# Seven block products instead of eight in a convolutional feed-forward down-projection, on one core

## The reference, cut to what matters

```
def conv_ffn(xn, buf, w_up, conv_w, conv_b, w_down):
    gu = xn @ w_up                       # (576, 1024) @ (1024, 6144)
    g, u = gu[..., :D_FF], gu[..., D_FF:]
    gc, new_buf = causal_dwconv(g, buf, conv_w, conv_b)   # width 3
    return (jax.nn.silu(gc) * u) @ w_down, new_buf        # (576, 3072) @ (3072, 1024)
x = x + conv_ffn(rmsnorm(x), ...)
```

## Time and profile before

| | |
|---|---|
| median of 3 runs | 1947.13 us (1945.86 to 1948.13) |
| the profiled execution | 1946.94 us, its span 1945.1 us |
| busy, PE / DVE / ACT / POOL | 98% / 55% / 39% / 36% |
| mean granted TensorE clock | 0.997 of full |
| loads and stores | 131.47 MB, mean 68 GB/s |

### The profile page before, as it was taken

How to read it: one execution, slowest core, us unless ns; L and a number is a source line. 1 busy time by engine, 2 the same in 40 slices (tenths; PEclk the granted TensorE clock), 3 DMA queues, 4 the chain that set the end, 5 groups by cost and what they waited for, 6 DMA issues and landing times.

```text
span 1945.1 us, 36321 instructions
## 1 busy us (share of the span) xinstructions
PE 1910.0 (98%) x13285; PEld 1840.1 (95%) x13285; DVE 1071.3 (55%) x1846; ACT 757.0 (39%) x1508; POOL 701.3 (36%) x688
## 2 busy tenths in 40 slices
PE   7999999999999999999999999999989999999998
PEld 7886679999999999999999999999989999999998
DVE  3677755556555655478435325439855852542541
ACT  4555655555455554331112111247653211121121
POOL 3340013433222233443333333366544343333331
PEclk9999999999999999999999999999999999999999
DMA  5320001311111110223322223232222322322222
GB/s 149 66 56 3 25 23 44 81 35 38 44 38 37 32 46 26 71 77 86 85 78 86 82 81 86 81 104 77 66 73 77 87 80 83 86 78 84 86 76 91
DMA packets 253078, 131.47 MB, mean 68 GB/s; under 512 B 43073, under 2 KB 250754, under 8 KB 252882
## 3 DMA queue, kind: packets, MB, share of 16 engines
q1 hardware_dynamic: 252514, 128.56, 23.8%
q10 hardware_dynamic: 444, 1.29, 0.2%
HBM read 126.21 MB, written 3.61 MB: 67 GB/s over the span
## 4 chain that ended last, share of the span: by engine, by line
PE 86%; DVE 9%; ACT 2%; issue 2%; DMA 1%; DVEq 0%; POOL 0%; SPq 0%; ACTq 0%; POOLq 0%
PE ps L200 18%; PE ps L203 18%; PE ps L201 17%; PE ps L1225 7%; PE ps L1223 7%; PE ps L1224 7%; PE ps L1253 3%; PE ps L999 2%; PE ps L1190 2%; DVE arena L1867 1%; PE ps L232 1%; PE ps L1026 1%; PE ps L1015 1%; DVE arena L2123 1%; DVE split L1870 1%
## 5 line engine op out<-in xcount | busy, mean ns | idle before, releaser
L200 PE MATMUL ps<-split,whi 128*128 128x288 f32 x3024 | 889.4, 296 | 11.1 <-DVE split L273 4.3
L201 PE MATMUL ps<-split,whi 128*128 128x288 f32 x3024 | 885.6, 295 | 0.0
L203 PE MATMUL ps<-split,wlo 128*128 128x288 f32 x3024 | 856.2, 295 | 0.0
L194 POOL TENSOR_TENSOR wlo<-raw,whi 128x1024 fp32r<-128x1024 f32 x187 | 457.3, 2447 | 615.1 <-ACT whi L171 604.5
L200 PEld LDWEIGHTS ps<-split,whi 128*128 128x128 f32 x3024 | 568.8, 188 | 15.2 <-issue 11.9
L201 PEld LDWEIGHTS ps<-split,whi 128*128 128x128 f32 x3024 | 569.0, 188 | 0.4
L203 PEld LDWEIGHTS ps<-split,wlo 128*128 128x128 f32 x3024 | 556.2, 188 | 0.0
L171 ACT CAST whi<-raw 128x1024 fp32r<-128x1024 f32 x187 | 194.8, 1043 | 378.3 <-DMA raw<-in_ffn_w_up 225.9
L1223 PE MATMUL ps<-split,split 128*128 128x384 f32 x768 | 268.3, 349 | 0.0
L1473 DVE TENSOR_REDUCE ssq<-arena 128x16 f32<-128x1024 f32 x128 | 156.2, 1220 | 186.7 <-ACT arena L1335 186.7
L1225 PE MATMUL ps<-split,split 128*128 128x384 f32 x768 | 258.0, 336 | 0.0
(11 more groups left out here) (285 smaller groups left out, 2107.7 us busy)
## 6 DMA issues: line engine op xcount, KB each, us to landing
raw<-in_ffn_w_up SPq DMA_DIRECT2D x96, 512.0 KB, 3.7
raw<-in_ffn_w_down SPq DMA_DIRECT2D x48, 512.0 KB, 3.9
arena<-in_cache_ckv SPq DMA_DIRECT2D x128, 128.0 KB, 2.0
raw<-in_rec_w_in SPq DMA_DIRECT2D x16, 512.0 KB, 3.8
raw<-in_attn_w_o SPq DMA_DIRECT2D x8, 512.0 KB, 4.9
raw<-in_rec_w_out SPq DMA_DIRECT2D x8, 512.0 KB, 4.0
raw<-in_attn_w_down SPq DMA_DIRECT2D x7, 512.0 KB, 7.6
raw<-in_attn_w_uq SPq DMA_DIRECT2D x48, 64.0 KB, 2.1
```

Of the source, the lines that this page charges most:

```text
L194: pool.tensor_tensor(wlo[:, t % RING, :], raw[:, t % RING, :], f32(whi[:, t % RING, :]), ALU.subtract).then_inc(w_lo, 1)
L200: pe.matmul(o, wh, a, start=first, stop=False)
L201: pe.matmul(o, wh, b, start=False, stop=False)
L203: mm = pe.matmul(o, wl, a, start=False, stop=last)
```

## The change

The down stage takes its 8 tiles in 4 pairs. A pair is a product of 2 x 2 blocks: two output chunks by two halves of the eight inner chunks (`HK` = 4 each) against those halves by two token halves. Instead of eight block products of 12 matmuls it makes seven (Strassen's scheme in Winograd's form), out of sums of weight blocks and sums of `h` blocks:

- DVE makes four sums of weight blocks per pair (`pair_sums`), ACT their high parts (`pair_high`), DVE the low parts of three of them (`sums_low`), and POOL the low parts of the four half tiles that are used as they are or in place (`pair_low`).
- DVE makes four differences and sums of `h` per round (`first_operands`, `second_operands`), ACT the high parts of all seven, DVE the low parts. Before, DVE made both parts itself.
- PE runs the seven products in three banks (`pair_pe`); DVE adds a bank to `xT` while PE goes on, in 288-column adds, seven per pair (`pair_add`). The products of pair 0 that need the last round's `h` are put last.
- The order of the inner chunks in the up stage changes (a round makes chunk r and chunk r + 4), the sums of pair 0 stand in the last round of the up stage, and the loops over rounds on ACT and DVE are written out.
- Outside the block: the gate weights of the recurrent layer are loaded two tiles later and split behind that layer's first norm; `frow` moves; three semaphores are shared with others.

The diff, cut to its core (lines that are only "..." stand for what is left out):

```
+        def pair_of(l, t0, s, p):
+            return t0 + 16 + 2 * (p % 2), s * 6 + p // 2, l * PAIRS + s * 4 + p
...
+        def pair_sums(dve, l, t0, s, p):
+            t, it, n = pair_of(l, t0, s, p)
+            b = p % 2
+            dve.wait_ge(w_loaded[t % RING], loaded(t) + 16 * it)
+            dve.wait_ge(w_loaded[(t + 1) % RING], loaded(t + 1) + 16 * it)
+            a11, a12 = first_half(raw, t), second_half(raw, t)
+            a21, a22 = first_half(raw, t + 1), second_half(raw, t + 1)
+            dve.tensor_tensor(s_raw[b][:, 0, :], a21, a22, ALU.add).then_inc(f_sum, 1)
+            dve.tensor_tensor(a21, a11, a21, ALU.subtract).then_inc(f_sum, 1)
+            dve.wait_ge(f_sum, SUM0 + 4 * n + 1)
+            dve.tensor_tensor(s_raw[b][:, 1, :], s_raw[b][:, 0, :], a11, ALU.subtract).then_inc(f_sum, 1)
+            dve.wait_ge(f_sum, SUM0 + 4 * n + 3)
+            dve.tensor_tensor(s_raw[b][:, 2, :], a12, s_raw[b][:, 1, :], ALU.subtract).then_inc(f_sum, 1)
+        def pair_high(act, l, t0, s, p):
+            t, it, n = pair_of(l, t0, s, p)
+            b = p % 2
+            split_hi(act, t, it)
+            act.wait_ge(f_sum, SUM0 + 4 * n + 3)
+            if b == 0:
+                act.copy(s_hi0[:, 0:2, :], s_raw[b][:, 0:2, :]).then_inc(f_hi, 1)
+            else:
+                act.copy(s_hi1, s_raw[b][:, 0:2, :]).then_inc(f_hi, 1)
+            act.wait_ge(f_sum, SUM0 + 4 * n + 4)
+            act.copy(s_hi(b, 2), s_raw[b][:, 2, :]).then_inc(f_hi, 1)
+            split_hi(act, t + 1, it)
+        def pair_low(pool, l, t0, s, p):
+            t, it, n = pair_of(l, t0, s, p)
+            def half_low(half, u, s_):
+                pool.tensor_tensor(half(wlo, u), half(raw, u), f32(half(whi, u)), ALU.subtract).then_inc(s_, 1)
+            pool.wait_ge(f_sum, SUM0 + 4 * n + 4)
+            pool.wait_ge(w_hi, t + 1 + 4 * it)
+            half_low(first_half, t, f_lo)
+            pool.wait_ge(w_hi, t + 2 + 4 * it)
+            half_low(first_half, t + 1, f_lo)
+            half_low(second_half, t, w_lo)
+            half_low(second_half, t + 1, w_lo)
+        def sums_low(dve, l, t0, s, p):
+            t, it, n = pair_of(l, t0, s, p)
+            b = p % 2
+            for i in range(3):
+                dve.wait_ge(f_hi, HI0 + 2 * n + (1 if i < 2 else 2))
+                dve.tensor_tensor(s_lo_op[b][:, i, :], s_raw[b][:, i, :], f32(s_hi(b, i)), ALU.subtract).then_inc(f_slo, 1)
+        def pair_product(pe, bank, wh, wl, op, ks, first, last, resumed=True):
+            wh, wl = wh.rearrange("p (k n) -> p k n", n=P), wl.rearrange("p (k n) -> p k n", n=P)
+            for k in ks:
+                mm = product(pe, [ps[:, bank, 0:HT]], wh[:, k, :], wl[:, k, :], [t_hi_op[:, k, op, :]],
+                             [t_lo_op[k][:, op, :]], first and k == 0, last and k == HK - 1, resumed)
+            return mm
+        def pair_pe(pe, l, t0, s, p, between=None):
+            t, it, n = pair_of(l, t0, s, p)
+            b = p % 2
+            x, y, z = X_BANK[b], Y_BANK, Z_BANK
+            h0 = l * FC + s * TF
+            every = range(HK)
+            a11, a12 = [first_half(v, t) for v in (whi, wlo)], [second_half(v, t) for v in (whi, wlo)]
+            s3, a22 = [first_half(v, t + 1) for v in (whi, wlo)], [second_half(v, t + 1) for v in (whi, wlo)]
+            s1, s2, s4 = [(s_hi(b, i), s_lo_op[b][:, i, :]) for i in range(3)]
+            def up_done(k, second):
+                if p == 0:
+                    pe.wait_ge(S["h"], h0 + 2 * k + 1 + second)
+            up_done(HK - 1, False)
+            pe.wait_ge(f_lo, LO0 + 2 * n + 1)
+            pe.wait_ge(acc_free[1], (t + AOFF) // 2 + 2 * it) if b == 0 else \
+                pe.wait_ge(acc_free[0], (t + 1 + AOFF) // 2 + 2 * it)
+            pair_product(pe, x, *a11, B11, every, True, True, False).then_inc(f_ps, 1)
+            pe.wait_ge(f_slo, SLO0 + 3 * n + 1)
+            if b:
+                pe.wait_ge(f_ev, EV0 + 5 * n - 1)
+            pair_product(pe, z, *s1, T1, every, True, True, False).then_inc(f_ps, 1)
+            early = range(HK - 1) if p == 0 else every
+            up_done(HK - 2, True)
+            pe.wait_ge(f_slo, SLO0 + 3 * n + 2)
+            pe.wait_ge(f_ev, EV0 + 5 * n + 1)
+            mm = pair_product(pe, x, *s2, T2, early, False, True)
+            if p == 0:
+                pe.wait_ge(w_lo, t + 1 + 4 * it)
+                pe.wait_ge(acc_free[0], (t + 1 + AOFF) // 2 + 2 * it)
+                pair_product(pe, y, *a12, B21, early, True, False, False)
+                pe.wait_ge(f_slo, SLO0 + 3 * n + 3)
+                pe.wait_ge(f_ev, EV0 + 5 * n + 2)
+                pair_product(pe, z, *s4, B22, early, False, False)
+                up_done(HK - 1, True)
+                mm = pair_product(pe, x, *s2, T2, range(HK - 1, HK), False, True)
+            mm.then_inc(f_ps, 1)
+            if between:
+                between()
+            pe.wait_ge(f_slo, SLO0 + 3 * n + 3)
+            pe.wait_ge(f_ev, EV0 + 5 * n + 2)
+            pair_product(pe, z, *s4, B22, range(HK - 1, HK) if p == 0 else every, False, True).then_inc(f_ps, 1)
+            pe.wait_ge(f_lo, LO0 + 2 * n + 2)
+            pe.wait_ge(f_ev, EV0 + 5 * n + 3)
+            pair_product(pe, x, *s3, T3, every, False, True).then_inc(f_ps, 1)
+            pe.wait_ge(w_lo, t + 1 + 4 * it)
+            if b == 0:
+                pe.wait_ge(acc_free[0], (t + 1 + AOFF) // 2 + 2 * it)
+            pair_product(pe, y, *a12, B21, range(HK - 1, HK) if p == 0 else every, p != 0, True, False).then_inc(w_used, 1)
+            pe.wait_ge(w_lo, t + 2 + 4 * it)
+            pe.wait_ge(f_ev, EV0 + 5 * n + (5 if b == 0 else 4))
+            pair_product(pe, x, *a22, T4, every, False, True).then_inc(w_used, 1)
+        def pair_add(dve, l, t0, s, p, then=None):
+            t, it, n = pair_of(l, t0, s, p)
+            b = p % 2
+            x, y, z = X_BANK[b], Y_BANK, Z_BANK
+            def add(i, j, bank, sem_):
+                v = xT[:, 2 * p + i, j * HT:(j + 1) * HT]
+                dve.tensor_tensor(v, v, ps[:, bank, 0:HT], ALU.add).then_inc(sem_, 1)
+            dve.wait_ge(f_ps, PS0 + 5 * n + 1)
+            add(0, 0, x, f_ev)
+            dve.wait_ge(f_ps, PS0 + 5 * n + 2)
+            add(1, 1, z, f_ev)
+            dve.wait_ge(f_ps, PS0 + 5 * n + 3)
+            add(0, 1, x, f_ev)
+            if then:
+                then()
+            dve.wait_ge(f_ps, PS0 + 5 * n + 4)
+            dve.wait_ge(f_ev, EV0 + 5 * n + 3)
+            add(0, 1, z, acc_free[1] if b else f_ev)
+            dve.wait_ge(f_ps, PS0 + 5 * n + 5)
+            add(1, 1, x, f_ev)
+            if p < 3:
+                sums_low(dve, l, t0, s, p + 1)
+            dve.wait_ge(w_used, t + 1 + 4 * it)
+            add(0, 0, y, f_ev if b else acc_free[0])
+            dve.wait_ge(w_used, t + 2 + 4 * it)
+            add(1, 0, x, acc_free[1 - b])
...
+                with pe.Fori(1 if s == 0 else 0, 4) as r:
+                    up(s, r, False)
+                for p in range(4):
+                    last = l == 1 and s == THIRDS - 1
+                    pair_pe(pe, l, t0, s, p, (lambda: fill(p)) if last else None)
...
                 for j in range(2):
                     t, it = t0 + 2 * j, s * 6 + r
-                    f = l * FC + s * TF + r * 2 + j
-                    split_hi(act, t + LEAD, it)
+                    if not (last and j):
+                        split_hi(act, t + LEAD, it)
                     if first and j == 0:
                         norm_root(act, i)
-                    split_hi(act, t + LEAD + 1, it)
-                    act.wait_ge(S["conv"], f + 3)
+                    if not (last and j):
+                        split_hi(act, t + LEAD + 1, it)
+                    act.wait_ge(S["conv"], l * FC + s * TF + r * 2 + j + 3)
                     act.activation(cb[:, j, 0:CBN], cb[:, j, 0:CBN], ACT.Silu).then_inc(S["silu"], 1)
-
-            def down(s, r):
...
+                    if last and j:
+                        pair_high(act, l, t0, s, 0)
+                    act.wait_ge(f_raw, RAW0 + 6 * R + (3 if j else 1))
+                    if j == 0:
+                        act.copy(hi[:, B11, :], hf[:, 0, 0:HT]).then_inc(f_cast, 1)
+                        act.wait_ge(f_raw, RAW0 + 6 * R + 2)
+                        act.copy(hi[:, T1, :], t_raw_at(r, T1, 1)).then_inc(f_cast, 1)
+                    else:
+                        act.copy(hi[:, B21:B22 + 1, :], hf[:, 1, :].rearrange("p (a n) -> p a n", a=2)).then_inc(f_cast, 1)
+                        act.wait_ge(f_raw, RAW0 + 6 * R + 6)
+                        act.copy(hi[:, T3:T4 + 1, :], t_raw_at(r, T3, 3)).then_inc(f_cast, 1)
...
+            for s in range(THIRDS):
+                if s == 0:
+                    up(0, 0, True)
+                for r in range(1 if s == 0 else 0, 4):
+                    up(s, r, last=r == 3)
+                for p in range(4):
+                    t, it, n = pair_of(l, t0, s, p)
```

(49 more changed lines are left out.)

209 lines of the change are left out of this document (104 added, 105 removed).

## The result

The changed kernel takes **2007.51 us** (median of four runs, 2005.51 to 2011.49; before, beside it, 1947.6): a ratio of 1.0312, 95% interval 1.0294 to 1.0330. Forecast were 2000.0 and a range of 1966 to 2032. Seven block products for eight cost 3% where 2% were to be saved.

What follows compares the result with a forecast made beforehand. PE was taken as the bound, busy 98% of the span, so fewer matmuls save time and pauses lose it. -38.1 + 82.2 + 7 + 2 + 1 - 0.7 = +53 on 1946.9 gives 2000 us, range 1966 to 2032.

Steps and rivals of the forecast that it cites:

- The saving: Down stages: seven block products for eight leave out 288 matmuls of 0.1323 us on PE, 38.1 us saved.
- Step 1: Entry of each down stage: PE waits 7.4 us for DVE's low part of a weight sum, then 1.5 at lowered clock.
- Step 2: Inside the pairs: PE waits for DVE's adds, 1.9 us in pair 0 and 2.9 a stage before odd pairs.
- a stage's sum: Each down stage loses 7.4 + 1.5 + 1.9 + 2.9 = 13.7 us, bounds 9.4 and 15.7; six stages 82.2.
- Step 3: First up thirds: DVE falls behind, so each layer's first down stage starts late; 7 us for both layers, bounds 0 and 10.
- Step 4: The rest: norm's low parts in layer 0's last stage 2 us, moved gate weights' split 1, tile 16's wait -0.7.
- (a): Down stages: POOL's halves fall between DVE's instructions, no turns; 9.4 us lost a stage, +22, 1969 us; chance 0.2.
- (c): Pair 0 of down stages: PE finds the weight sum's low part in time; faster than before, 1938 us; chance 0.06.

Runs made afterwards that it cites:

- the kernel with all moves: Changed kernel with pair_high, sums_low(0), pair 0's first two adds, the y add and pair 1's sums all moved earlier: 1956.23 us, ratio 1.0042.
- the kernel with the adds early: Changed kernel with pair_high and sums_low(0) moved earlier and pair 0's first two adds put behind the last h difference: 1983.22 us, ratio 1.0184.

## Why the prediction was right, step by step

**The saving** was 38.1 forecast, 38.8 by itself. The trace's 0.1323 a matmul held. By the formula of the Trainium skill ("TensorE: Matmul & The Clock Gate", section "Wait — 56ns, not 53.3ns?") the estimate would have been 35.3; the runs are nearer to the trace.

**Step 1, the pause and the clock.** T1 was put 9.0 us behind the last up product and came 8.7 behind it (1108.77, less the 1100.08 at which a next product would have started, 0.13 behind 1099.95). The pause before T1 and B11's wait make 6.7 for 7.4, the half clock 1.8 for 1.5. Mechanism and place were right, the turns by three instructions too. One part was off: the h multiply was not held (0.76), the instructions behind it were. And of the two rows given for reads that are not held, only the second shows it: at 850.20 POOL's instruction had not begun (851.10).

**Step 2.** T3 and T4 lost 1.27 for 1.9, the odd pairs 1.99 and 1.56 for 1.7 and 1.2. The reason given was right but not the whole of it: with the y add moved, the pause at pair 3 passed on to T2, and it went only when the low parts were parted.

**What a stage's sum left out.** 11.5 of pauses and 1.8 of clock are 13.3, and 14.9 were lost. Of the rest, 1.6, some 1.4 are six restarts: the matmul that ends a stretch runs 0.29 where its successor would have begun 0.13 after it, and the one that begins the next takes 0.37 for 0.29, together 0.24 a pause that no wait in the profile holds. So 13.7 a stage was up to 1.2 too low. (The lower bound of 9.4 a stage holds the clock at 1.5, though its own bound was 0; with 0 it would have been 7.9.)

**Step 3, the lag of the first thirds, was wrong:** 7 us forecast for the two layers, at most 0.4 found. T1 came 8.69 behind where a next product was due in the first stage (947.51 for 938.82), as in the later ones of the layer, and 9.1 behind it in the first stage of layer 1 (1621.61 for 1612.51). From the norm's matmul (840.66) to where B11 of the first stage was due (938.82) are 98.2; before, to the end of the last up product (944.35 less a tile's 6.35) 98.8. I had read the 86 of 102 us of VectorE as its load. The kernel with loops written out shows that 21 of 82 us go with the loop alone, and the stretch after the change has 71: some 10 us of work added, 21 taken away by the same edit. That VectorE therefore stayed level with PE is the likely reason; the kernel after with its loops kept was not run.

**Step 4.** The norm in layer 0's last stage cost more than its 2: that layer grew by 31.7, three stages of 8.5 are 25.5, which leaves 6. In that stage T4 waits in pairs 1, 2 and 3 too, for 0.6, 1.77 and 1.79 us, as it does in no other. The stretch between the layers, where the gate weights' split moved, grew by 2.7 for 1. The +1.5 ahead of the first norm I had not forecast, and its cause was not sought.

So the misses cancel in part: some 5 us too few in the stages (those of the second layer are a little shorter), 7 too many in the lag, 4 too few at the norm, 4 elsewhere. That the total came within 8 us owes something to this. The place, the price and the cause of the loss were right.

**Rivals.** (a), no turns, was run for step 1 alone, as the kernel with `pair_high` moved: 1993, not 1969. It had the pause at its bound (4.83) and the fall of the clock that the rival's 9.4 holds (0.50 from 1102 to 1104). What it did not have are the rival's low waits in the pairs, 3.0 us a stage: they stayed at 32.9 us, since POOL's halves of the later pairs still fell among the low parts. The restarts, the norm and the 1.5 ahead of it make up most of the rest. (c) needed the order on VectorE not to be what the code says; when the order was rewritten to that end, the kernel was faster than before by 18 us.

## What to carry to other kernels

A saving on the busiest engine is counted in a moment; what decides is the list of the engine that now feeds it at the hand-over between two stages. Write down, for that engine, what the busy one needs and by when, and put the list in that order: moving one late item can pass the pause on to the next at no gain, or at a loss where the clock falls once more (2018 and 2002 us), or win what it promised where nothing waits close behind (1987), while ordering all of them, and parting the long ones, turned +3.1% into -0.9% with no work removed. Where a third engine holds the feeding one's instructions, its own work is better placed ahead of the hand-over: that alone gave 13 to 15 us here.

## What was unexpected of the hardware

- **Loops.** With waits and addresses from registers, in a loop, VectorE is busy for 81.9 us of the stretch shown above; with the same code written out for 60.5, and the kernel's time is the same. A dependent instruction starts 0.04 behind its source (848.38 to 848.42) instead of 0.16:

```profile
847.80 0.58 DVE L1850 TENSOR_SCALAR arena<-arena,fpar 128x592 f32<-128x592 f32 x1
848.42 0.83 DVE L1852 SCALAR_TENSOR_TENSOR arena<-arena,fpar 128x592 f32<-128x592 f32 x1
```

and most of the 21 us are time in which GpSimd's instructions held it. The h multiply, the groups of the same stretch by line, in the loop and written out:

```profile
L1867 DVE TENSOR_TENSOR arena<-arena,work 128x576 f32<-128x576 f32 x7 | 20.9, 2986 | 0.2
```

```profile
L1867 DVE TENSOR_TENSOR arena<-arena,work 128x576 f32<-128x576 f32 x7 | 9.3, 1327 | 0.2
```

In the loop every one of the seven takes 2.98 to 3.00, for 0.76 of work. So a busy share of 85% on VectorE (81.9 of 96) can hold much waiting that sits inside its records. Why the two engines fall out of step with the loop written out was only read from the trace, not tried.

- **The clock after a pause of 2.9 us.** In the kernel with all moves it fell behind the pause of 2.87 (0.50 from 1100 to 1102). In the kernel with the adds early it stayed at 1.00 behind one of 2.85 that ended at 1101.99:

```profile
1102.00:1104.00 2.00, 2.00 (x15) 2.00 (x16) 1.84 (x3) 1.38 (x2) 0.00 (x0) 1.00 0.00 0
```

The same kernel's pause of 2.85 in the first stage did lower it (0.50 from 944 to 946), and in the second stage it fell later, at 1114, behind a pause of 2.00, where the kernel after kept 1.00 behind 1.99. A pause of 2 to 3 us can thus cost its clock or not; what decides was left open.
